# Two weight buffers made into one, 16 bytes into it: TensorE's moving operands at 208 instead of 192 bytes above the weights, modulo 256

## What is computed

```
def first_block(...):                     # adaptive norms, latent attention beside a short convolution
    qa_l, kva_l, kr_l, cb_l, cc_l, ch_l = split_projection(h_l @ w_in[l])
    ...
    x = x + gt_a * merge_heads(att_l, conv_l, g_mix_out[l], w_out[l])
    x = x + gt_f * conv_ffn(hf_l, w_up[l], ffn_conv_w[l], ffn_conv_b[l], w_down[l])   # width 2 x 5504
    return rms_norm(x, g_final)

def second_block(...):                    # block-sparse attention beside forgetting attention
    z = hn @ w_in
    ...
    merged = jax.nn.sigmoid(g_a) * a + jax.nn.sigmoid(g_b) * bfx
    x = x + merged @ w_out
    x = x + jnp.square(jax.nn.relu(hm @ w_up)) @ w_down                              # width 8192
    return rms_norm_2(x, norm_final_g)
```

## Time and profile before

| | |
|---|---|
| median of two runs | 2751.22 us |
| the profiled execution's own time | 2751.76 us |
| its span, from first to last instruction | 2749.9 us |
| mean granted TensorE clock | 0.98 of full |
| TensorE matmuls busy | 2646.2 us, 96% of the span |
| TensorE weight loads busy (they overlap the matmuls) | 2561.8 us, 93% |
| VectorE / ScalarE busy | 63% / 45% |
| matmuls | 21,440 |
| bytes moved by DMA | 553.56 MB |

### The profile page before, as it was taken

The page is one execution under the profiler, slowest core; times in us unless marked ns, Lnnn a source line. Parts: engine busy times, 40 slices in busy tenths (PEclk is TensorE's granted clock), DMA queues, the critical chain, the costliest instruction groups (busy, mean ns, idle before and its releaser), DMA issues.

```text
span 2749.9 us, 51222 instructions
## 1 busy us (share of the span) xinstructions
PE 2646.2 (96%) x21440; PEld 2561.8 (93%) x21440; DVE 1738.6 (63%) x2020; ACT 1224.0 (45%) x1487; POOL 102.9 (4%) x196
## 2 busy tenths in 40 slices
PE   6899988889999999999999999999999999999998
PEld 4699768789999999999999999999999999999997
DVE  5988676778887655665565555555555555555554
ACT  6743333334445543444543444444444444434433
POOL 0000323300000000000000010000000000000000
PEclk9999989999999999999999999999999999999999
DMA  9878665757776555565654555665556666666662
GB/s 358 273 239 270 224 207 188 235 202 246 256 249 215 184 195 174 170 212 172 187 177 146 154 161 161 192 193 191 184 182 192 194 193 196 192 193 191 197 208 100
DMA packets 289064, 553.56 MB, mean 201 GB/s; under 512 B 19386, under 2 KB 28712, under 8 KB 288232
## 3 DMA queue, kind: packets, MB, share of 16 engines
q1 hardware_dynamic: 288328, 548.53, 62.5%
q10 hardware_dynamic: 544, 2.29, 0.2%
HBM read 548.53 MB, written 2.10 MB: 200 GB/s over the span
## 4 chain that ended last, share of the span: by engine, by line
PE 84%; DVE 9%; ACT 2%; issue 2%; DMA 1%; POOL 1%; SPq 0%; ACTq 0%; DVEq 0%; POOLq 0%
PE half L1868 25%; PE half L1869 25%; PE half L1870 25%; DVE wlo L1092 3%; DVE acc L1121 1%; DMA raw<-in_w_ada 1%; ACT whi L612 1%; PE half L1902 1%; PE half L1904 1%; PE half L1903 1%; DVE acc L1124 1%; PE half L2161 1%; PE half L1991 0%; PE half L2122 0%; PE half L2149 0%
## 5 line engine op out<-in xcount | busy, mean ns | idle before, releaser
L1092 DVE TENSOR_TENSOR wlo<-raw,whi 128x1024 fp32r<-128x1024 f32 (+1 forms) x909 | 1091.1, 1211 | 837.1 <-ACT whi L612 834.6
L612 ACT ACTIVATE whi<-raw 128x1024 fp32r<-128x1024 f32 (+1 forms) x909 | 942.0, 1048 | 1080.0 <-PE half L1870 956.6
L1868 PE MATMUL half<-hf,whi 128*128 128x256 f32 x2400 | 669.4, 279 | 9.2 <-DVE hf L1184 5.2
L1869 PE MATMUL half<-hf,whi 128*128 128x256 f32 x2400 | 667.5, 278 | 0.0
L1870 PE MATMUL half<-hf,wlo 128*128 128x256 f32 x2400 | 667.5, 278 | 0.0
L1868 PE MATMUL half<-hid,whi 128*128 128x256 f32 x1712 | 476.8, 278 | 0.0
L1869 PE MATMUL half<-hid,whi 128*128 128x256 f32 x1712 | 476.1, 278 | 0.0
L1870 PE MATMUL half<-hid,wlo 128*128 128x256 f32 x1712 | 476.1, 278 | 0.0
L1868 PEld LDWEIGHTS half<-hf,whi 128*128 128x128 f32 x2400 | 452.3, 188 | 11.3 <-issue 5.8
L1870 PEld LDWEIGHTS half<-hf,wlo 128*128 128x128 f32 x2400 | 454.4, 189 | 0.0
L1869 PEld LDWEIGHTS half<-hf,whi 128*128 128x128 f32 x2400 | 451.8, 188 | 0.0
(11 more groups left out here) (284 smaller groups left out, 3055.7 us busy)
## 6 DMA issues: line engine op xcount, KB each, us to landing
raw<-in_w_up SPq DMA_DIRECT2D x288, 512.0 KB, 4.4
raw<-in_w_in SPq DMA_DIRECT2D x216, 512.0 KB, 3.8
raw<-in_w_down SPq DMA_DIRECT2D x212, 512.0 KB, 4.6
raw<-in_w_ada SPq DMA_DIRECT2D x192, 512.0 KB, 5.2
raw<-in_w_out SPq DMA_DIRECT2D x64, 512.0 KB, 4.8
raw<-in_w_proj_a SPq DMA_DIRECT2D x16, 512.0 KB, 3.8
raw<-in_w_proj_b SPq DMA_DIRECT2D x16, 512.0 KB, 4.0
raw<-in_w_up SPq DMA_DIRECT2D x16, 384.0 KB, 3.5
```

The source lines that it names most:

```text
L612: A(whi[:, s, 0:elems], raw[:, c, 0:elems], ACT.Copy).then_inc(s_hi_ready, 1)
L1092: V.tensor_tensor(wlo[:, s, 0:elems], raw[:, c, 0:elems], whi[:, s, 0:elems].bitcast(F32), ALU.subtract).then_inc(s_drained, 1)
L1868: mm(o, hi, x[:, 0:T], start=(k == 0 and b % 2 == 0), stop=False, skip_group_check=True)
L1869: mm(o, hi, x[:, T:2 * T], start=False, stop=False, skip_group_check=True)
```

## The change

The two weight buffers become one, `splits`, of 2 x 4 x 1024 + 8 elements. `whi` and `wlo` are views into it that start 4 elements (16 bytes) from its beginning. The buffer is 32 bytes longer than the two were, and every tile declared after it moves up by 32 bytes.

```
-        whi = sb("whi", [P, NSPLIT, CW], F32R)
-        wlo = sb("wlo", [P, NSPLIT, CW], F32R)
+        splits = sb("splits", [P, 2 * NSPLIT * CW + 8], F32R)
+        whi, wlo = [splits[:, 4 + i * NSPLIT * CW:4 + (i + 1) * NSPLIT * CW].rearrange("p (s n) -> p s n", s=NSPLIT) for i in range(2)]
```

## The result

The changed kernel takes 2839.97 us (two runs, 2839.21 and 2840.72) against 2751.22 before: a ratio of 1.0322, 95% interval 1.0297 to 1.0347. It is slower by 89 us, 15 us beyond the upper end of the range. The profiled execution has a span of 2837.4 us.

What follows compares the result with a forecast made beforehand. The prediction took TensorE's distance between matmul starts to bound the kernel. Four effects of place, each put at 0, summed to 0 against the profiled 2751.8 us, giving 2750 us with a range of 2692 to 2825.

Steps and rivals of the forecast that it cites:

- What bounds the kernel: TensorE, busy 96% of the span: time is gained or lost by the distance from one matmul's start to the next.
- Two rhythms, chosen at restarts: Equal TensorE matmuls run 117.8 or 113.3 ns apart for hundreds of microseconds, changing only where something comes between products.
- two streams that find their own phase: Weight loads and moving operands on TensorE settle again after the 16-byte shift: 0 us, bounded by 70 less and 160 more.
- A straddling weight block: Weight blocks touching one more unit of memory on TensorE: taken as 0, with 13 us kept for the range.
- ScalarE and VectorE at 16 bytes off: The engines' splits using the shifted buffer cost nothing: 0, at most 3 us for VectorE before 900 us.
- Streamed tiles at 32 modulo 64: Everything declared later moves by 32 bytes, so streamed tiles start there: 0.
- D: Rival, chance 0.23: all TensorE matmuls in the slow rhythm, 51 us more, or one 4.4 ns step slower, 136 more.
- slow rhythm: TensorE matmul starts 117.8 ns apart; 7,800 matmuls were counted to it before the change.
- A: The forecast case, chance 0.50: both rhythms stay on TensorE, their shares too or nearly; own range 2725 to 2785 us.
- B: Rival, chance 0.14: the quick rhythm everywhere on TensorE, 30 us off 2751, about 2720 us.
- C: Rival, chance 0.13: less contention than in either rhythm, distances 111.5 to 112.3 ns, 70 to 54 us less.
- quick rhythm: TensorE matmul starts 113.3 ns apart; 11,500 matmuls were counted to it before the change.

Runs made afterwards that it cites:

- w160_m96: Weights and streamed tiles both 32 bytes higher than in the kernel before; relation (streamed start less weight start, modulo 256) still 192; 2744.74 us, ratio 1.0000.
- w128_m192: Against the kernel before, weights stay at 128 modulo 256 and streamed tiles start at 192, relation 64; 2804.14 us, ratio 1.0212.
- w144_m80: Weights and streamed tiles both 16 bytes higher than in the kernel before, relation still 192; 2724.84 us, ratio 0.9926.
- w176_m112: Weights and streamed tiles both 48 bytes higher than in the kernel before, relation still 192; 2721.48 us, ratio 0.9913.
- w128_m96: Against the kernel before, only the streamed tiles move, up by 32 bytes, relation 224; 2811.37 us, ratio 1.0239.
- w128_m48: Against the kernel before, weights stay and streamed tiles start at 48 modulo 256, relation 176, 16 bytes below 192; 2825.78 us, ratio 1.0286.
- w128_m80: Against the kernel before, weights stay and streamed tiles go to 80 modulo 256, relation 208 as in the change; 2806.06 us, ratio 1.0217.
- hid_m96: The kernel before with 32 bytes laid ahead of the two hidden tiles only, streamed at relation 224, others at 192; 2761.86 us, ratio 1.0052.
- w176_m128: Weights and streamed tiles both 32 bytes away from the changed kernel's addresses, relation 208 as there; 2846.60 us, ratio 1.0371.

## Why the prediction was wrong, point by point

**What bounds the kernel: right.** The whole difference is in the distance of matmuls that wait for nobody, and the two splitting engines only wait longer.

**Two rhythms, chosen at restarts: right for relation 192, and the most useful reading.** w160_m96 drew them anew, one stretch quick that was slow before, at the same time in all. The rows of `kvn` gave relation 64 the same two rhythms, and w128_m192 bears that out. But they said nothing of how often each comes (117.8 ns in all of its long stretches, 59 us more), and nothing of relations that are no multiple of 64. I let them stand for all relations.

**The failing step: "two streams that find their own phase ... should find it again. I take no change in the length of either rhythm".** This term was put at 0 and is the whole 89 us. The rhythms belong to the relation: the change has no 113.3 ns, and 123.3 ns in its place over the longest stretch. w160_m96, w144_m80 and w176_m112 have other addresses and relation 192 and keep 113.3; w128_m96, w128_m48 and w128_m80 have the weights of before and another relation, and lose it. hid_m96 does it to one tile alone. The bounds of this term, 70 us less and 160 more, held. What I made of them did not: I chose a value on an argument about settling that no row supported, and then cut the range at 2825, halfway into the only rival that lay above it.

**A straddling weight block, 0 with 13 us kept: too small, and the sign is not fixed.** At relation 192 a start at 16 modulo 32 takes 20 to 24 us off (w144_m80, w176_m112); at 208 it puts 34 to 41 us on (w176_m128 or the change against w128_m80). Rows 10 and 11 showed only that the weight load alone pays nothing. As said above, the moving operand's start changes along with it.

**ScalarE and VectorE at 16 bytes off, 0: right.** 1212 against 1211 ns, 1048 against 1048.

**Streamed tiles at 32 modulo 64, 0: right by itself.** w160_m96 has them there and takes the time of before.

**The rivals.** D, slower everywhere, was right in its place, its sign and its threshold. Up to the second feed-forward the slow rhythm or just above it is nearly all there is, 30 us more. Its next step, 4.4 ns above 117.8, came as 5.5, in the second feed-forward and briefly before. So the 89 us lie between its 51 and its 136. Its reason, one more piece touched by each stream, is refuted: w144_m80 has both streams off a multiple of 32 and is faster than before. Of A the slow rhythm stayed and the quick one did not; B and C did not come here, though B is what w176_m112 is: the quick rhythm everywhere, 24 us less where B had 30.

**The rule of the Trainium skill.** The Trainium skill's page "SBUF — State Buffer", section "A bandwidth-pool intuition that's wrong (but worth ruling out)", gives LDWEIGHTS an independent read port. I took that to mean that the relation of two addresses cannot matter. The runs span 0.991 to 1.037 on places alone, so the measurement decides against this reading for split float32 operands of 256 columns. Of the 109.2 ns, the estimate by the Trainium skill's page "TensorE: Matmul & The Clock Gate", section "Wait — 56ns, not 53.3ns?", no run came nearer than 113.3 with 256 columns.

**Left open.** Why the start within 32 bytes matters, and whether it is that of the weight block or of the moving operand. Whether one element off 192 is slow by its relation or by weights off a multiple of 16. What the two streams meet at: a collision of reads was not ruled out by any run, but nothing here shows one. Relations from 68 to 156 and from 4 to 60 were not tried, nor most of those between the ones that were.

## What to carry to other kernels

Where TensorE loads new weights for every 256 streamed columns and waits for nobody, read the distance between starts in the long stretches, window by window: two values for equal instructions mean that something other than work sets the pace. Then try a few placements of the streamed tiles against the weights, 16 bytes at a time, and hold that relation fixed when tiles are added; 32 bytes more ahead of the streamed tiles cost this kernel 2.4% (w128_m96). Where a term of the sum rests on no row at all, its range must reach both bounds.

## What the hardware showed that was not expected

- Equal matmuls in long stretches ran at 113.3, 116.7, 117.3, 117.7, 118.3, 118.7, 119.2, 120.0 and 123.3 ns, at the full clock and with no wait. The addresses decide which of these values can come, and no long stretch was below 113.3.
- Of ten relations modulo 256, only 192 and 64 have the 113.3 ns: the moving operand 64 bytes to either side of the weights, modulo 256. At 64 with weights at 0 modulo 32 it lasts only some 10 us at a time. With operands one element (4 bytes) off 192 a matmul takes 4.4 to 10 ns more than 113.3.
- With weights at 16 modulo 32 and relation 192 every long stretch is in the quick rhythm; with 0 modulo 32 some stay at 117.8 ns for hundreds of microseconds.
- The turn from one rhythm to another with the operand (hid_m96) takes a few matmuls and needs no pause.
